# Twelve modulation chunks summed by the vector engine, and keys and values of the latent attention in split form

## The reference

```python
for i in range(DEPTH_2):
    sh1, sc1, g1, sh2, sc2, g2 = jnp.split((silu_c @ mod_w[i] + mod_b[i])[:, None, :], 6, axis=-1)
    csh1, csc1, cg1, csh2, csc2, cg2 = jnp.split(silu_cctx @ mod_w[i] + mod_b[i], 6, axis=-1)
```

```python
kv = (rms_norm(kv_lat, kv_norm_g) @ w_kv_up).reshape(b, n, MLA_HEADS, MLA_NOPE + MLA_V)
k_nope = rms_norm(kv[..., :MLA_NOPE], kn_nope_g)
v = kv[..., MLA_NOPE:]
```

## Time and profile before

| what | value |
| --- | --- |
| median of three runs | 1846.36 us (1841.34 to 1850.29) |
| profiled execution | 1847.99 us |
| its span in the trace | 1846.2 us |
| tensor engine busy | 1708.6 us, 93% |
| vector engine busy | 1132.2 us, 61% |
| ScalarE, GpSimd busy | 31%, 32% |
| the head | up to some 229 us |
| keys, values and queries of the latent attention | 1473.9 to 1555.2 us |

### The profile page before, as it was taken

The page is one execution under the profiler, slowest core; times in us unless marked ns, Lnnn a source line. Parts: engine busy times, 40 slices in busy tenths (PEclk is TensorE's granted clock), DMA queues, the critical chain, the costliest instruction groups (busy, mean ns, idle before and its releaser), DMA issues.

```text
span 1846.2 us, 24761 instructions
## 1 busy us (share of the span) xinstructions
PE 1708.6 (93%) x9774; PEld 1321.0 (72%) x9774; DVE 1132.2 (61%) x2078; ACT 579.5 (31%) x918; POOL 584.9 (32%) x570
## 2 busy tenths in 40 slices
PE   6999999998879888799869888999999999999999
PEld 6876688876537356567536656989999745589997
DVE  4334357877687787767787667575553326635554
ACT  4444433211121212111211113443333445634332
POOL 0111100777657676557767761000000100000000
PEclk9998999999999999899989989999999999999999
DMA  7998875999999999999999995845555323035553
GB/s 274 317 324 286 285 267 187 409 409 409 409 401 390 409 409 408 398 362 408 408 409 409 409 401 183 279 145 183 182 182 163 95 67 102 1 114 183 182 183 136
DMA packets 223420, 515.93 MB, mean 279 GB/s; under 512 B 13324, under 2 KB 122204, under 8 KB 223324
## 3 DMA queue, kind: packets, MB, share of 16 engines
q0 software_dynamic: 86784, 318.80, 44.5%
q1 hardware_dynamic: 136192, 195.71, 31.0%
q10 hardware_dynamic: 348, 0.11, 0.0%
HBM read 513.53 MB, written 1.05 MB: 279 GB/s over the span
## 4 chain that ended last, share of the span: by engine, by line
PE 59%; DMA 22%; DVE 9%; POOL 5%; issue 3%; ACT 2%; SPq 0%; DVEq 0%; POOLq 0%
DMA more<-in_peer_v_dram,idx 12%; PE bank L920 9%; PE bank L923 9%; PE bank L921 9%; DMA more<-in_peer_u_dram,idx 6%; POOL more L814 5%; PE bank L1282 4%; PE wide L1334 4%; PE wide L1069 2%; DVE more L2503 2%; DMA weights<-in_w_in_dram 2%; PE bank L874 1%; PE wide L1607 1%; PE bank L1561 1%; PE bank L995 1%
## 5 line engine op out<-in xcount | busy, mean ns | idle before, releaser
L2112 DVE TENSOR_TENSOR low_weights<-weights,high_weights 128x2048 fp32r<-128x2048 f32 x107 | 245.1, 2292 | 314.3 <-ACT high_weights L1716 314.0
L2503 DVE CUSTOM_DVE_ANT_0 more<-more,wide 128x1024 f32<-128x1024 f32 x256 | 310.8, 1219 | 152.9 <-DMA more<-in_peer_u_dram,idx 150.7
L920 PE MATMUL bank<-high_input,high_weights 128*128 128x256 f32 x1264 | 360.7, 285 | 7.1 <-DVE low_input L2112 7.0
L921 PE MATMUL bank<-high_input,low_weights 128*128 128x256 f32 x1296 | 364.6, 281 | 0.0
L923 PE MATMUL bank<-low_input,high_weights 128*128 128x256 f32 x1264 | 357.3, 283 | 0.0
L814 POOL DMA_INDIRECT more<-in_peer_u_dram,idx x256 | 285.4, 1115 | 198.1 <-DVE dots L2503 88.9
L1334 PE MATMUL wide<-more,rstd 128*128 128x512 f32 x476 | 243.0, 646 | 78.0 <-ACT rstd L1904 60.5
L1716 ACT ACTIVATE high_weights<-weights 128x2048 fp32r<-128x2048 f32 x107 | 204.7, 1914 | 304.2 <-DMA weights<-in_ffn_w_gate_dram 78.8
L814 POOL DMA_INDIRECT more<-in_peer_v_dram,idx x256 | 253.7, 991 | 115.3 <-issue 68.7
L920 PEld LDWEIGHTS bank<-high_input,high_weights 128*128 128x128 f32 x1264 | 239.4, 189 | 16.7 <-issue 16.3
L921 PEld LDWEIGHTS bank<-high_input,low_weights 128*128 128x128 f32 x1296 | 249.0, 192 | 0.5 <-issue 0.5
(11 more groups left out here) (296 smaller groups left out, 2313.7 us busy)
## 6 DMA issues: line engine op xcount, KB each, us to landing
weights<-in_ffn_w_down_dram SPq DMA_DIRECT2D x33, 1024.0 KB, 4.9
weights<-in_ffn_w_gate_dram SPq DMA_DIRECT2D x30, 1024.0 KB, 5.5
weights<-in_ffn_w_up_dram SPq DMA_DIRECT2D x30, 1024.0 KB, 5.4
weights<-in_conv_w_in_dram SPq DMA_DIRECT2D x24, 1024.0 KB, 9.2
weights<-in_w_in_dram SPq DMA_DIRECT2D x20, 1024.0 KB, 9.9
nrm<-in_mod_w_dram POOLq DMA_DIRECT2D x14, 1024.0 KB, 8.7
sq<-in_mod_w_dram POOLq DMA_DIRECT2D x13, 1024.0 KB, 7.2
h_ctx<-in_mod_w_dram POOLq DMA_DIRECT2D x13, 1024.0 KB, 6.8
```

The lines of the kernel that those rows point to most:

```text
L920: first = nc.tensor.matmul(out, cut(high), hi, start=start, stop=False, **more_args)
L921: nc.tensor.matmul(out, cut(w_lo[b]), hi, start=False, stop=False, **more_args)
L2112: return nc.vector.tensor_tensor(out, a, b, op)
L2503: nc.vector.tensor_tensor_reduce(u, u, wide[0][:, :], 1.0, 0.0, ALU.mult, ALU.add, dots[:, n % 16:n % 16 + 1]).then_inc(s_dot, 1)
```

## The change

In the head, chunks 6, 8, 10, 12, 18, 20, 22, 24, 30, 32, 34 and 36 (`VECTOR_MODS`, the second chunk of beats 0 to 3, 6 to 9 and 12 to 15) hold the four parts of quads 8, 9 and 10 (`VECTOR_QUADS`), and the vector engine sums them: for each of a chunk's two row blocks it multiplies 128x1024 weights by a column of the silu of `c` and adds it into `mod_sum` (new, in `more`). It does so at the end of its beat s+1 for the chunk of beat s. The tensor engine adds over the partitions and turns with eight matmuls a quad in beats 5, 11 and 17 (`mod_turn_sum`). The other 36 chunks (`TENSOR_MODS`) hold quads 0 to 7 and 11 and stay where they were; their copies and turns are counted by rank among them (`mod_rank`). POOL's load j waits for the vector engine's addition where chunk j-3 is one of the twelve. Quads 8, 9 and 10 (the first gate and the second shift and scale of the second layer) are used for the tokens alone, so only the vector `c` is summed.

In the latent attention, the three weight chunks of keys and values are brought to split form, with keys and values apart (`kv_w_hi`, `kv_w_lo`, laid over `h_ctx`, `nrm` and `big`), and so is `kvlat` (`kvlat_hi`, `kvlat_lo`). A pair's keys are now six fp32r matmuls of 512 columns into all 128 rows, its values six of 512 or twelve of 256 columns. ScalarE makes the high halves of the weights behind `high("mla_q", 2)`, behind pair 1 and within the last query quad, the vector engine the low halves at the same places.

```diff
+VECTOR_BEATS = [0, 1, 2, 3, 6, 7, 8, 9, 12, 13, 14, 15]
+VECTOR_MODS = [FIRST + 2 * _s for _s in VECTOR_BEATS]
+TENSOR_MODS = [_j for _j in range(48) if _j not in VECTOR_MODS]
+TENSOR_QUADS = list(range(8)) + [11]
+VECTOR_QUADS = [8, 9, 10]
+VECTOR_TURNS = {5: 8, 11: 9, 17: 10}
...
 def turned_after(j):
-    return [(j - 5) // MOD_PARTS] if j >= 5 and j % MOD_PARTS == 1 else []
+    if j in VECTOR_MODS:
+        return []
+    n = mod_rank(j)
+    return [(n - 5) // MOD_PARTS] if n >= 5 and n % MOD_PARTS == 1 else []
...
@@ gpsimd, loads of the modulation
+                elif j >= 3 and j - 3 in VECTOR_MODS:
+                    pool.wait_ge(s_mod_added, VECTOR_MODS.index(j - 3) + 1)
                 elif j >= 3:
-                    pool.wait_ge(s_mod_used, j - 2)
-                quad, part = j // MOD_PARTS, j % MOD_PARTS
+                    pool.wait_ge(s_mod_used, mod_rank(j - 3) + 1)
+                quad, part = mod_part(j)
...
@@ tensor
+            def mod_turn_sum(quad):
+
+                pe.wait_ge(s_mod_added, MOD_PARTS * (VECTOR_QUADS.index(quad) + 1))
+                wait_free(pe, "mod_turn", quad)
+                b = bank_of("mod_turn", quad)
+                for m in range(8):
+                    mm = nc.tensor.matmul(bank[b][:, 2 * m:2 * m + 2], mod_sum[:, m * P:(m + 1) * P], ones[:, 0:2],
+                                          start=True, stop=True)
+                mm.then_inc(full[b], 1)
...
-                for j in beat_mods(s)[:1]:
+                for j in tensor_mods(s, True):
                     mods(j)
...
-                for j in beat_mods(s)[1:]:
+                for j in tensor_mods(s, False):
                     mods(j)
+                for quad in vector_turns(s):
+                    mod_turn_sum(quad)
...
-            pe.wait_ge(s_kvlat, 2)
+            pe.wait_ge(s_kvlat_lo, 2)
...
                 for k in range(2):
-                    for h in range(2):
-                        mm = nc.tensor.matmul(b[NOPE * h:NOPE * h + NOPE, :], wt[:, k, 2 * (n - pairs[0]) + h, 0:NOPE],
-                                              kvlat[:, k, :], start=(k == 0), stop=(k == 1))
+                    for i, (wt, x) in enumerate(((high, kvlat_hi), (low, kvlat_hi), (high, kvlat_lo))):
+                        at = 2 * NOPE * (n - pairs[0])
+                        mm = nc.tensor.matmul(b[:, :], wt[:, 0, k, at:at + 2 * NOPE], x[:, k, :],
+                                              start=(k == i == 0), stop=(k == 1 and i == 2))
...
-                        mm = nc.tensor.matmul(b[:, MV * heads * a:MV * heads * (a + 1)], kvlat[:, k, t * P:(t + 1) * P],
-                                              wt[:, k, :, NOPE:P], start=(k == 0), stop=(k == 1))
+                        for i, (x, wt) in enumerate(((kvlat_hi, high), (kvlat_hi, low), (kvlat_lo, high))):
+                            mm = nc.tensor.matmul(b[:, MV * heads * a:MV * heads * (a + 1)], x[:, k, t * P:(t + 1) * P],
+                                                  wt[:, 1, k, :], start=(k == i == 0), stop=(k == 1 and i == 2))
...
@@ scalar
             high("mla_q", 1)
...
             side_root("kv_ones")
+            for k in range(2):
+                act.wait_ge(s_kvlat, k + 1)
+                nc.scalar.activation(kvlat_hi[:, k, :], kvlat[:, k, :], ACT.Copy).then_inc(s_kvlat_hi, 1)
             side_root("kpe_mean")
             high("mla_q", 2)
+            high_kv(0)
...
             for n in range(KV_FIRST):
                 kv_pair(n)
+                if n == 1:
+                    high_kv(1)
...
@@ vector
+            def add_modulation(j):
+
+                quad, part = mod_part(j)
+                v.wait_ge(m_landed[j % 3], 16 * (j // 3 + 1))
+                if part == 0 and quad > VECTOR_QUADS[0]:
+                    wait_full(v, "mod_turn", quad - 1)
+                for k in range(2):
+                    rows, by = mod_w[j % 3][:, k, :], cvec[:, 2 * part + k, 0:1]
+                    if part == k == 0:
+                        settle(nc.vector.tensor_scalar(mod_sum, rows, by, None, ALU.mult))
+                    else:
+                        settle(nc.vector.scalar_tensor_tensor(mod_sum, rows, by, mod_sum, ALU.mult, ALU.add))
+                v.sem_inc(s_mod_added, 1)
+
+            v.wait_ge(s_cvec, 3)
             for s in range(HALVES + 1):
                 if s < HALVES:
                     front(s)
...
                 if s in BEAT and BEAT[s] + 3 < 20:
                     low("qkv", BEAT[s] + 3)
+                for j in vector_mods(s - 1) if s >= 1 else []:
+                    add_modulation(j)
...
             for n in range(KV_FIRST):
                 kv_pair(n)
+                if n == 1:
+                    low_kv(1)
```

More of the change, by code:

```diff
@@ L1063, in mod_chunk @@
                     pe.wait_ge(m_landed[j % 3], 16 * (j // 3 + 1))
[L1064 to L1065 removed]
+                if part == 0 and rank:
+                    pe.wait_ge(s_mod_left, rank)
                 for k in range(2):
@@ L1493, in _ @@
                                                            start=True, stop=True))
-            pe.wait_ge(s_kvlat, 2)
+            pe.wait_ge(s_kvlat_lo, 2)
             def kv_pair(n):
-                s, pairs = next(x for x in KV_CHUNKS if n in x[1])
+                c = next(i for i in range(3) if n in KV_CHUNKS[i][1])
+                s, pairs = KV_CHUNKS[c]
                 heads = 2 * len(pairs)
-                wt = ring[slot_of("heads", s)][:, 0:2 * P * heads].rearrange("p (k h c) -> p k h c", k=2, h=heads)
+                _, _, slot, count, size = kv_chunk(c)
+                high, low = (a[c][:, :].rearrange("p (c k n) -> p c k n", c=2, k=2) for a in (kv_w_hi, kv_w_lo))
                 if n == pairs[0]:
-                    wait_weights(pe, "heads", s)
+                    pe.wait_ge(w_split[slot], count)
                 wait_free(pe, "kv", 2 * n)
@@ L2026, in _, with high_kv @@
             high("mla_q", 1)
+            def high_kv(c):
+                stage, s, b, _, size = kv_chunk(c)
+                wait_weights(act, stage, s)
+                raw = ring[b][:, 0:size].rearrange("p (h n) -> p h n", n=P)
+                high = kv_w_hi[c][:, :].rearrange("p (c h n) -> p c h n", c=2, n=NOPE)
+                for part in range(2):
+                    last = nc.scalar.activation(high[:, part], raw[:, :, NOPE * part:NOPE * part + NOPE], ACT.Copy)
+                last.then_inc(w_high[b], 1)
             side_root("kv_ones")
+            for k in range(2):
+                act.wait_ge(s_kvlat, k + 1)
+                nc.scalar.activation(kvlat_hi[:, k, :], kvlat[:, k, :], ACT.Copy).then_inc(s_kvlat_hi, 1)
             side_root("kpe_mean")
             high("mla_q", 2)
+            high_kv(0)
             for s in range(3):
@@ L2594, in _, with low_kv @@
                 scaled(kvlat[:, k, :], kvlat[:, k, :], vcol("kv_lat", k), root).then_inc(s_kvlat, 1)
+            for k in range(2):
+                v.wait_ge(s_kvlat_hi, k + 1)
+                tt(kvlat_lo[:, k, :], kvlat[:, k, :], kvlat_hi[:, k, :].bitcast(F32), ALU.subtract).then_inc(s_kvlat_lo, 1)
+            def low_kv(c):
+                _, _, b, count, size = kv_chunk(c)
+                v.wait_ge(w_high[b], count)
+                raw = ring[b][:, 0:size].rearrange("p (h n) -> p h n", n=P)
+                high = kv_w_hi[c][:, :].bitcast(F32).rearrange("p (c h n) -> p c h n", c=2, n=NOPE)
+                below = kv_w_lo[c][:, :].rearrange("p (c h n) -> p c h n", c=2, n=NOPE)
+                for part in range(2):
+                    last = tt(below[:, part], raw[:, :, NOPE * part:NOPE * part + NOPE], high[:, part], ALU.subtract)
+                last.then_inc(w_split[b], 1)
             root = inverse_root("kpe_mean")
```

89 lines of the change are left out of this document (63 added, 26 removed).

## The result

| | before | after |
| --- | --- | --- |
| median | 1845.74 us (four runs, 1841.34 to 1850.29) | 1963.57 us (four runs, 1961.67 to 1967.29) |
| ratio | | 1.0624, 95% interval 1.0601 to 1.0646 |
| span of the profiled execution | 1846.2 us | 1959.9 us |
| start to the output projections (the head) | 228.7 us | 346.3 us |
| first key matmul to the queries' rope (six pairs) | 30.4 us | 26.2 us |

The kernel became 118 us slower. The head takes 117.6 us more, keys and values 3.6 us less, and all other stretches together differ by 0.3 us. The page after, to be held against the earlier trace rows: the busy line, the tensor engine's tenths, its clock, and the transfers.

What follows compares the result with a forecast made beforehand. The tensor engine, busy 93% of the span, was taken to bound the kernel. 1848.0 + 111 (head: waits and low clock) - 7 (keys and values) = 1952 us; 1950 predicted, as the runs' median is 1.6 lower; range 1918 to 1996.

Steps and rivals of the forecast that it cites:

- The ring (part 2): Head: modulation loads wait for late vector additions, which wait on weight chunks; head +87 us before any low clock.
- the lap of 20.5 us at full clock: Head, gated beats: weight chunk, copies, high half, low half, addition, load, modulation matmuls take 20.5 us instead of 9.70.
- from the scores: Head, beats 13 to 16: no low half; front 1.1, back 2.4, addition 2.6, load 5.7, matmuls 1.0 to 2.0 us.
- The clock: Head: tensor engine at about half rate after waits, 2.65 us for each of nine bursts, +24; bounds 0 to +46.
- B: Rival, head: the same waits close but the clock stays full, 24 us less, 1926 us; chance 0.17.
- C: Rival, head: all tensor work between the waits runs at 1.2 GHz, +42 us more, 1992 us; chance 0.15.
- A: Main case, head: waits close on every gated beat, clock falls for part of each burst, 1950 us; chance 0.63.
- The end of the head: Last stretch to the output projections: the last quad's turn takes +86.4 to +87; head +111 with the low clock.
- Part 1: Head, tensor engine alone: twelve modulation chunks leave (12.0 us), three turns cost 2.9 us more; -9.1 us.
- The additions' price: Head, vector engine: a chunk's two summing instructions of 128x1024 add 2.6 us to each gated beat.
- Keys and values: Latent attention: split matmuls take a pair from 4.64 to 3.67 us; -7 us taken, bounds -7.8 to 0.
- of its copies only the one behind pair 1 (1.2 us) can show: Keys and values: ScalarE has 2.5 us of work a pair against a pitch of 3.67, so 0 to 1 us shows.

Runs made afterwards that it cites:

- the run with fillers: Changed kernel plus 26 matmuls of constants in the tensor engine's wait in each of nine gated beats; ratio 1.0639 to the kernel before, head 344.5 us.
- the trace with the clock nearly up: Changed kernel plus matmuls of constants fitted in number (26, 12 or 20) to the tensor engine's waits; ratio 1.058 to the kernel before, head 330.6 us.
- that half alone: Kernel before with only keys and values in split form, all modulation on the tensor engine; ratio 0.9981, -4.0 us.

## Why the prediction was right

1950 us were predicted, 1963.57 measured, within the range of 1918 to 1996. The prediction's own sum was 1952 for the profiled execution; that took 1961.67. The head came 6.6 us higher than forecast and keys and values gave 3.4 less, so the two misses add up and do not cancel. The range had its upper end from its terms (1950 + 22 + 18 + 7 = 1997); by the same terms the lower one is 1925, and no row gives 1918. By its steps:

**The ring (part 2).** It closed where it was placed and, up to beat 11, with the members it was given; the lap of 20.5 us at full clock was 20.7 in the run with fillers. The openings of the weight chunks, worked out at full clock, then with 2.65 us for each burst behind a wait up to there, against the trace:

| beat | full clock | with the clock | measured |
| --- | --- | --- | --- |
| 2 | 98.7 | 101.4 | 101.2 |
| 5 | 163.0 | 173.6 | 173.2 |
| 8 | 204.5 | 217.8 | 217.0 |
| 11 | 255.2 | 273.8 | 273.9 |
| 14 | 281.9 | 303.1 | 305.8 |
| 16 | 303.6 | 327.5 | 330.6 |

Within 1 us up to beat 11 with the clock, some of it by luck: the head's first chunk opened 1.3 us later than in the trace of before (70.01 against 68.70), and the table counts a burst's 2.65 us in full at the opening behind the wait, where at beat 2 only the modulation chunk's 0.94 of them have passed. Ten waits were seen, eleven forecast. At beat 14 the ring was not the forecast one, "from the scores" without a low half:

```profile
285.26 1.81 ACT high_weights L1790
...
295.63 0.76 DVE more L2422
```

The last low half, of beat 11, began at 287.09 behind a high half that had waited for the turned probabilities, and then the vector engine did the softmax work of two heads before it came to the addition. The 2.7 us by which beat 14 opened late stand there; this is read from the chain and not tested.

**The clock.** +24 for nine bursts; 30 by the windows above, seven bursts at 2.2 to 3.2 and two at 7.5 and 5.0, less the 5 us that the low stretch at 160.8 had cost the kernel before. That this comes out at 25 is in part luck: a burst lost 3.4 us in the mean and not 2.65, and the 5 us to be taken off were not in the forecast. Rivals B and C fall: B by the 15.7 us that came back in the trace with the clock nearly up, so far as that one stretch carries; C because no burst stayed low throughout (the lowest, at 238.62, has a mean of 0.64, though by its length it lost 7.5 us, as much as C gives to each). C's price of +66 in all also lay above the prediction's own bound of +46 for the clock. The rule that was weighed (the Trainium skill, TensorE: Matmul & The Clock Gate, HAM oscillation) is that the burst behind each wait starts at half rate, and the traces agree: all nine bursts began at the lower level, 1.93 or 1.94 us for the chunk's matmuls. But it says how a burst starts, and A starts so too. What made C was the further step that all work in the ring is slow, and in most laps the clock rose within the weight chunk.

**The end of the head** is where the missing 6.6 us lie (+117.6 against +111). Three had come up by beat 16. From there to the output projections it took 15.7 us instead of 11.5 (the head ended at 228.7 before): the weight chunk behind the last wait ran 8.1 us (330.64 to 338.77), low at first, not 5.8, and the last summed quad's turn (1.95 us) fell there as a whole. The prediction had given 0.6 us to this stretch; the 2.65 for its burst are in the 327.5 of the table already.

**Part 1** (-9.1 us on the tensor engine) was never measured by itself: where the ring is closed, what the tensor engine saves makes its wait longer by as much, as the order of the chain has it. The additions' price of 2.6 us a lap is 2.51 on the chain.

**Keys and values** were mis-sized: -7 forecast, -3.6 in the traces, -4.0 by the ratio of that half alone. The matmuls are as worked out; a pair's pieces on the chain after are

```profile
1609.63 0.86 PE wide L1605 x2
1610.49 1.39 PE bank L1580 x6
1611.88 1.43 PE bank L1592 x12
```

3.68 us where 3.67 had been expected and 4.64 had been. So the eight pairs gave 7.8. Two new waits took 3.6 of that, and the first product behind each of them ran some 0.25 longer (1.67 and 1.64 us for a pair's keys instead of 1.39). The step that failed is "of its copies only the one behind pair 1 (1.2 us) can show": it went through ScalarE's copies and not through the order on the vector engine. There the six scalings of query latents, which stand ahead of pair 0's keys, hold back a bank (1.3 us), and the last low half stands behind a rotation that itself waits for the tensor engine (2.3 us):

```profile
1657.51 0.42 DVE L2206 TENSOR_TENSOR sq<-wide,consts 128x256 f32<-128x256 f32 x1 [5.64 <-PE wide L1611]
...
1660.03 1.29 DVE L2206 TENSOR_TENSOR low_kv_weights<-weights,high_kv_weights 128x512 fp32r<-128x512 f32 x2
```

The vector engine was idle for 5.64 us, up to 1657.51, although the high half that the low half needs had ended at 1653.0: the low half is written behind the rotation. It is the head's mistake in small. The cause of the 2.3 us is shown by the run that moved it; that of the 1.3 us is read from the wait alone.

## What to carry to other kernels

Work moved to an idle engine costs what its place in that engine's order costs: ask when the instruction can start, who waits for its end, and how many beats of slack the shared buffer gives, before asking how long it is. A buffer that two engines release hands the slower one's lag to the faster one through the queue that loads it, and the loss (here 92 us) is there even if the moved work is empty. A mark with no work of its own can also be set before the instruction ahead of it has ended, so such a test is not the same ring with one member less. Where such a wait comes back every lap, add the low clock of the burst behind it to the bill.

## What the runs showed of the hardware

- An fp32 `scalar_tensor_tensor` of 128x1024 on the vector engine takes 1.28 us, `tensor_scalar` of the same shape 0.75, and the first over 64 columns 0.285: by these two widths about 0.22 us are fixed, which is an estimate.
- Keeping the tensor engine busy with constants in its waits raised the mean granted clock of the stretch with the waits from 0.74 to 0.94 and made the head 15.7 us shorter in the trace, although it added some 80 us of work to the tensor engine.
- The low clock came without a wait too: 18.1 us at 0.62 in that run, from 269.80 on, behind 10 us of work without a gap at 1.00.
- A semaphore step written behind a vector instruction of 2.29 us reached GpSimd 0.07 us after that instruction's start (109.67, 109.74), where nothing made it wait for the end.
- A modulation load of 1 MB landed after 5.5 to 5.8 us with little beside it, and after 8.6 and 10.3 us beside another and the weights.
